# A two-layer encoder with eight experts: one of three weight sums of the second expert matrix moves from VectorE to GpSimd

## What is computed

```python
def swiglu(h, w_gate, w_up, w_down):
    return (jax.nn.silu(h @ w_gate) * (h @ w_up)) @ w_down

def moe_swiglu(h, w_router, w_gate, w_up, w_down):
    logits = (h @ w_router).astype(jnp.float32)
    top_val, top_idx = lax.top_k(logits, TOP_K)
    top_w = jax.nn.softmax(top_val, axis=-1)
    combine = jnp.sum(jax.nn.one_hot(top_idx, N_EXPERTS, dtype=jnp.float32) * top_w[..., None], axis=-2)
    out = jnp.zeros(h.shape, jnp.float32)
    for e in range(N_EXPERTS):
        y = swiglu(h, w_gate[e], w_up[e], w_down[e]).astype(jnp.float32)
        out = out + combine[..., e:e + 1] * y
    return out.astype(h.dtype)
```

## Time and profile before

| what | value |
|---|---|
| median of 3 runs | 1532.44 us (1530.07 to 1533.12) |
| the profiled execution's own time | 1528.53 us |
| its span | 1526.7 us |
| mean granted clock of PE | 0.998 |
| PE busy | 1508.6 us, 99% |
| VectorE busy | 921.5 us, 60% |
| ScalarE busy | 497.4 us, 33% |
| GpSimd busy | 25.3 us, 2% |
| read from HBM | 471.38 MB |

### The profile page before, as it was taken

The page is one execution under the profiler, slowest core; times in us unless marked ns, Lnnn a source line. Parts: engine busy times, 40 slices in busy tenths (PEclk is TensorE's granted clock), DMA queues, the critical chain, the costliest instruction groups (busy, mean ns, idle before and its releaser), DMA issues.

```text
span 1526.7 us, 27999 instructions
## 1 busy us (share of the span) xinstructions
PE 1508.6 (99%) x11888; PEld 1033.6 (68%) x11888; DVE 921.5 (60%) x1533; ACT 497.4 (33%) x741; POOL 25.3 (2%) x39
## 2 busy tenths in 40 slices
PE   9999999999999999999999999999999999999997
PEld 7887788888888878843466566565565665664664
DVE  7778776888787776643824835726528339248211
ACT  5698745444457987420020110100100100201001
POOL 0000000000000000010000000000000000000100
PEclk9999999999999999999999999999999999999999
DMA  9544376555554444499999999999999999999994
GB/s 385 177 162 164 116 248 207 186 184 182 194 179 149 155 166 146 141 364 425 425 410 425 425 417 425 418 416 425 418 420 426 413 425 424 412 425 416 422 425 183
DMA packets 72673, 478.10 MB, mean 313 GB/s; under 512 B 8097, under 2 KB 8353, under 8 KB 45154
## 3 DMA queue, kind: packets, MB, share of 16 engines
q1 hardware_dynamic: 68656, 460.09, 75.8%
q0 software_dynamic: 3456, 15.72, 2.7%
q10 hardware_dynamic: 434, 0.45, 0.1%
HBM read 471.38 MB, written 4.85 MB: 312 GB/s over the span
## 4 chain that ended last, share of the span: by engine, by line
PE 85%; ACT 6%; DVE 5%; DMA 2%; issue 1%; SPq 0%; ACTq 0%; DVEq 0%
PE bank L1508 24%; PE mid L1508 12%; PE turn L1536 11%; PE bank L1233 7%; PE bank L1239 7%; PE bank L1242 7%; PE mid L1536 4%; PE mid L1233 2%; PE mid L1239 2%; PE mid L1242 2%; PE turn L1570 2%; ACT w_hi L586 1%; DVE w_lo L593 1%; DMA wide<-in_e_down 1%; PE mid L1345 1%
## 5 line engine op out<-in xcount | busy, mean ns | idle before, releaser
L1508 PE MATMUL bank<-wide,gT 128*32 128x448 f32 x3624 | 438.5, 539 | 0.0
L1508 PEld LDWEIGHTS bank<-wide,gT 128*32 128x32 f32 x3624 | 221.4, 110 | 131.6 <-issue 22.6
L593 DVE TENSOR_TENSOR w_lo<-raw,w_hi 128x1024 fp32r<-128x1024 f32 x202 | 244.4, 1223 | 93.0 <-ACT w_hi L586 90.6
L1508 PE MATMUL mid<-wide,gT 128*32 128x448 f32 x1824 | 254.2, 539 | 0.0
L586 ACT ACTIVATE w_hi<-raw 128x1024 fp32r<-128x1024 f32 (+1 forms) x202 | 210.2, 1053 | 101.1 <-PE bank L1242 65.5
L1145 ACT ACTIVATE eh<-bank 128x448 f32<-128x448 f32 x48 | 22.6, 544 | 478.3 <-PE bank L1508 478.3
L1536 PE MATMUL turn<-wide,hT 128*32 128x512 f32 x534 | 176.8, 592 | 1.4 <-DVE sums_w L2140 1.4
L1233 PE MATMUL bank<-w_hi,a_hi 128*128 128x512 f32 (+1 forms) x608 | 164.6, 394 | 0.8 <-ACT a_hi L869 0.8
L2219 DVE TENSOR_TENSOR eh<-mid,eh 128x448 f32<-128x448 f32 x32 | 19.8, 620 | 241.2 <-PE mid L1508 241.2
L1508 PEld LDWEIGHTS mid<-wide,gT 128*32 128x32 f32 x1824 | 115.5, 110 | 66.4 <-issue 12.8
L1242 PE MATMUL bank<-w_lo,a_hi 128*128 128x512 f32 (+1 forms) x608 | 157.1, 381 | 2.1 <-DVE w_lo L593 2.1
(11 more groups left out here) (313 smaller groups left out, 1985.0 us busy)
## 6 DMA issues: line engine op xcount, KB each, us to landing
wide<-in_e_in SPq DMA_DIRECT2D x227, 896.0 KB, 12.4
wide<-in_e_down SPq DMA_DIRECT2D x102, 1024.0 KB, 13.6
raw<-in_stream SPq DMA_DIRECT2D x100, 1024.0 KB, 4.8
extra<-in_e_in SPq DMA_DIRECT2D x23, 896.0 KB
extra<-in_e_down SPq DMA_DIRECT2D x10, 1024.0 KB
raw<-in_e_in SPq DMA_DIRECT2D x6, 896.0 KB, 4.5
wg<-in_gates POOLq DMA_DIRECT2D x2, 2048.0 KB, 10.5
table<-y_rows POOLq DMA_DIRECT2D x7, 384.0 KB
```

Of the source, the lines that this page charges most:

```text
L593: nc.vector.tensor_tensor(w_lo[:, h % H, :], raw[:, part % R, lo:lo + HALF], w_hi[:, h % H, :].bitcast(F32), ALU.subtract).then_inc(lo_rea ...
L1508: ins = nc.tensor.matmul((early, late)[m][t_][strip(r), 0:LANE_W], gT[:, kt, strip(t_)], w_[:, r * LANE_W:(r + 1) * LANE_W], start=kt == 0 ...
```

## The change

GpSimd's loop gets the last sum of each of the 14 parts, between its fetch and its store; VectorE's `weight_sums` loses it. Operands, target and semaphores stay the same.

```diff
@@ -824,6 +824,12 @@
                 if e:
                     pool.wait_ge(g_turned, TURNED_G * e)
                 fetch(FETCHES[0], e)
+                for d in range(N_DOWN):
+                    n = e * N_DOWN + d
+                    own_ = set_of(n)
+                    pool.wait_ge(w_second, n + 1)
+                    nc.gpsimd.tensor_tensor(own_[:, 3, :], weights_of(0, N_IN + d, e)[:, 2 * CB:3 * CB], own_[:, 2, :],
+                                            ALU.subtract).then_inc(w_sums, 1)
                 pool.wait_ge(row_dve, ROW_DVE * (e + 1))
                 pool.dma_start(table[1 + e * CAP:1 + (e + 1) * CAP, :], y_rows[0:CAP, :]).then_inc(row_stored, 16)
             pool.wait_ge(row_stored, 16 * EXPERTS)
@@ -2116,14 +2122,6 @@
 
                 def weight_sums(e, parts):
 
-                    def last_sum_of(d):
-                        n = e * N_DOWN + d
-                        own_ = set_of(n)
-                        w_ = weights_of(pas, N_IN + d, e)
-                        dve.wait_ge(w_second, n + 1)
-                        nc.vector.tensor_tensor(own_[:, 3, :], w_[:, 2 * CB:3 * CB], own_[:, 2, :],
-                                                ALU.subtract).then_inc(w_sums, 1)
-
                     for d in parts:
                         n = e * N_DOWN + d
                         own_ = set_of(n)
@@ -2134,12 +2132,9 @@
                             dve.wait_ge(w_sums_used, n - SETS + 1)
                         nc.vector.tensor_tensor(own_[:, 0:2, :], blocks[:, :, 1, :], blocks[:, 0, :, :],
                                                 ALU.subtract).then_inc(w_first, 1)
-                        if d > parts[0]:
-                            last_sum_of(d - 1)
                         dve.wait_ge(w_first, n + 1)
                         nc.vector.tensor_tensor(own_[:, 2, :], own_[:, 1, :], w_[:, 0:CB],
                                                 ALU.add).then_inc(w_second, 1)
-                    last_sum_of(parts[-1])
 
                 def turn_selection(n, e):
```

## The result

The changed kernel takes 1554.98 us (median of 4 runs, 1554.85 to 1555.14) against 1531.29 us before (4 runs). The ratio is 1.0162, 95% interval 1.015 to 1.0175: 24 us slower. The profiled executions differ by 26.2 us of span (1552.9 against 1526.7). Ratios and intervals leave out the one slow run on record, 2234.76 us at a granted clock of 0.655, in the experiment with the copy.

What follows compares the result with a forecast made beforehand. In the second matrix PE, VectorE and transfers were nearly full, with PE setting an expert's end. 35.4 - 1.3 = 34.1 us on the profiled 1528.5 gave 1562.6, or 1566.5 on the runs' median; range 1547 to 1590.

Steps and rivals of the forecast that it cites:

- (a): VectorE, expert stage: 98 last sums removed at 0.60 us each, 59 us in all, 8.4 an expert.
- (b): GpSimd, expert stage: 98 last sums added at 1.27 us each; their result by itself hardly a cost.
- (c): Second matrix: what VectorE and GpSimd do to each other makes a part 2.95 us, where it was 2.34.
- the row of turns: Second matrix: VectorE's pair, GpSimd's sum, then the third sum's tail, 1.13 + 1.27 + 0.55 us a part; chance 0.62.
- sharing: Rival, second matrix: both engines alternate element by element, 2.68 us a part, 1547.6 us; chance 0.12.
- (d): Second matrix: 6.1 us later over ten parts, 1.05 absorbed by slack; PE ends each expert 5.05 later, 35.4 in all.
- (e): Late experts: with PE slower the transfers get ahead again, giving back 1.3 us.
- (f): GpSimd's queue: the sums between an expert's fetch and store move neither against PE; program loading costs nothing.
- (g): First matrix, sums of parts 0 to 2: at most 3 x 1.27 us more against 4.67 of wait, so nothing.
- no collision: Rival, second matrix: the engines do not collide in a way that counts, 1530.6 us; chance 0.11.
- Worse turns: Rival, second matrix: GpSimd also loses or runs longer when interrupted, 3.29 us a part or more, 1590 us; chance 0.15.
- PE's clock: Second matrix: it could fall while PE waits half a microsecond a part; judged unlikely, no size or separate chance given.

Runs made afterwards that it cites:

- the experiment with the copy: Changed kernel, but GpSimd copies b21 into the last sum's place, one operand read and no subtraction: 1527.97 us, ratio 0.9983 to the kernel before.
- the run with writes: Changed kernel, but GpSimd writes zeros three times in the last sum's place and reads nothing: 1527.2 us, ratio 0.998 to the kernel before.
- parts 3 to 8: Changed kernel, but GpSimd makes the last sums of these six parts only, VectorE the others: 1547.28 us, ratio 1.012 to the kernel before.

## Why the prediction was right

Forecast 1566.5 us, measured 1554.98, inside 1547 to 1590; the sign and the mechanism were right, and one term was too large.

**(a), (b)**, what moves and its price: 98 instructions, 1.27 us each when nobody is in the way (minimum 1.27). Right. A late result by itself costs hardly anything: 1.75 us late did no harm in the run with writes, and 2.27 us late does not decide when PE ends an expert, as part 13 above shows.

**(c)**, the row of turns: right in its order, pair, GpSimd, third sum. Its size was the mis-sized term: 2.95 forecast, 2.82 measured. I had added start to start, whole length and tail. In fact GpSimd comes out 1.22 us behind the point where the pair lets go (849.98 + 1.13 = 851.11, to 852.33), since the first hundredths of its 1.27 pass while it waits, and the next pair starts 0.07 before the third sum's recorded end (852.80 against 852.87). 0.13 us x 10 parts x 7 experts is 9.1 us, of the 10.4 that lie between the forecast difference (34.1) and the measured one (23.7). With 2.82 the same sum reads 10 x 0.48 - 1.05 = 3.75 an expert and 25.0 in all. PE's first matmul of expert 7 moved from 1405.84 to 1431.26, 25.4 us.

The Trainium skill (SBUF — State Buffer, section Who interferes with whom) calls it an exclusive lock for the whole instruction. The runs agree. In the changed kernel a pair, that of part 1 in expert 1, that started 0.39 us into a sum of GpSimd's did nothing until that was over, and ended 1.09 us behind it, about the 1.13 that a pair holds VectorE:

```profile
832.55 1.97 DVE L2133 TENSOR_TENSOR sums_w<-wide 128x1024 f32<-128x1024 f32 x1 [0.47 <-DMA wide<-in_e_down]
```

```profile
832.16 1.27 POOL L831 TENSOR_TENSOR sums_w<-wide,sums_w 128x512 f32<-128x512 f32 x1 [46.16 <-DVE sums_w L2136]
```

With sharing as in my rival (0.64 of the overlap of 0.88 us) the pair would have taken 1.78. The same section of the Trainium skill (SBUF — State Buffer, section Who interferes with whom) exempts GpSimd instructions that only write, and VectorE instructions with at most one SBUF input outside the 2-port modes. The runs agree: a pair and a third sum kept 1.22 and 0.69 us beside GpSimd's writes, and a product with one operand in PSUM kept 0.62 beside its subtraction. The Trainium skill (SBUF — State Buffer, section A bandwidth-pool intuition that's wrong (but worth ruling out)) has a hand-over of some 115 ns, there for a transfer issued by GpSimd. It would have given an estimated 3.07 us a part and does not come on top here: the measured part, 2.82, is shorter even than my sum without it. Whether a hand-over is hidden inside the 1.22 us that GpSimd still needs behind a pair, no row tells.

**(d)**, slack: for all parts together 1.05 us at part 13 was the right figure, as the latest part decides. As a general rule it was wrong, and parts 3 to 8 showed it: the slack belongs to a part, and PE has next to none up to part 9 (by the part-by-part reckoning).

**(e)**, what comes back from the transfers: 1.3 forecast. The store of expert 6's rows moved by 25.4 us (1415.26 to 1440.68), the fetch ahead of it by 23.0 (1312.94 to 1335.94), so expert 6 lost 2.4 against 3.8 in the others: 1.4 back. Right.

**(f), (g)**, GpSimd's queue and the parts made ahead: right; VectorE waits 5.40 us for PE ahead of the products of expert 1 although the pair of part 1 took 1.97. Two records of a GpSimd configuration (MODIFY_POOL_CONFIG) stand at 668.7, just behind the first fetch, 50 us ahead of its first sum.

The rivals: sharing and no collision are excluded by the rows above; the first would have been 2.68 us a part. Worse turns did not come: in the row of turns GpSimd waits only behind the pair, and its record grows by no more than that wait. PE's clock stayed at 1.00.

Left open: the timed difference is 23.7 us and that of the profiled spans 26.2. Some 1 us of the latter lies behind PE's last matmuls, in the output (PE's L1593 at 1515.19 of 1526.7 before, L1599 at 1540.42 of 1552.9 after); the rest is likely the spread of the kernel before, whose medians beside the experiments, 1529.57 and 1529.79, lie 25.4 and 25.2 us under the changed kernel. It wasn't looked into further.

## What to carry to other kernels

Before work is moved from VectorE to GpSimd, list what VectorE does at the same time. Here its instructions with two SBUF operands and a GpSimd instruction that reads SBUF ran one after the other, so moving 0.60 us of such work brought 0.95 us of standing still. Count each in its turn, not on its engine; the profile showed this waiting as longer instructions and not as idle. A wait that shows up on PE, here 36.7 us for GpSimd's results, need not be the cost either: ask what the engine would have waited for next. GpSimd's work that only wrote, or that ran beside a VectorE instruction with a PSUM operand, was free. And when several paces stand within 1% of each other, as here PE and VectorE in the second matrix (2.36 and 2.34 us a part) and PE and the transfers over an expert (106.3 and 107.2), ask first what a perfect version would bring: here 2.4 us.

## What was not expected of the hardware

The loss is tight, at the two lengths tried: VectorE's third sum, issued just after GpSimd got in, grows by GpSimd's own length less 0.32 us (1.27 gives 0.95, 0.61 gives 0.29), and GpSimd's record grows by 0.92 to 0.94 behind a pair, for the subtraction and the copy alike. A pair that comes 0.39 us into GpSimd's 1.27 grows by 0.75. Of GpSimd's 128x512 float32 forms the subtraction takes 1.27 us, the copy 0.61 and the blanking 0.53. The form with two operands is the dear one, and its length is what a collision costs.
